# Moving a table build, two routings a tile and some opening work in a two-layer decoder kernel

## The reference, cut to what matters

```python
for l in range(2):
    h = rms_norm(x, norm1_g[l]);  q, k, v, f, u_pool, u_ssm = split(h @ w_in[l])
    att  = forgetting_attention(q, k, v, f)        # 8 heads x 64
    pool = multiscale_pool(u_pool)                 # windows 2, 4, 8, 16
    ssm  = s5(u_ssm)                               # 1024 complex states: s[t] = a*s[t-1] + b*u[t]
    x = x + concat(rms(att), rms(pool), rms(ssm)) @ w_out[l]
    h = rms_norm(x, norm2_g[l])
    for head in range(8):                          # "routing": product keys, top 16 of 128 x 128
        s1, s2 = scores(h @ w_q[l, head]);  e, gate = top16(top16(s1) + top16(s2))
        x = x + sum_k gate_k * gelu(h . u_tab[e_k]) * v_tab[e_k]
```

## Time and profile before

| what | value |
|---|---|
| median of 3 runs | 1547.77 us (1547.66 to 1549.18) |
| the profiled execution | 1547.98 us, of which span 1546.1 |
| busy: PE, DVE, ACT, POOL | 1049.1, 1083.2, 575.1, 619.7 us |
| moved by DMA | 623.55 MB, mean 403 GB/s |
| of that by the gathers' queue | 536.90 MB |

### The profile page before, as it was taken

One profiled execution on the slowest core, in us unless ns is written; L12 is line 12 of the kernel. 1 busy time (PEld: TensorE's weight loads), 2 busy tenths in 40 slices (PEclk: granted clock), 3 DMA queues, 4 the chain that ended last, 5 costly groups with the idle time before them and its releaser, 6 DMA issues. The chain is left out here.

```text
span 1546.1 us, 19439 instructions
## 1 busy us (share of the span) xinstructions
PE 1049.1 (68%) x6790; PEld 532.8 (34%) x6790; DVE 1083.2 (70%) x2485; ACT 575.1 (37%) x1768; POOL 619.7 (40%) x571
## 2 busy tenths in 40 slices
PE   8898656785854668776775667788588465565555
PEld 6685312333531334332552334333255111111111
DVE  8777998646999685654789767564579965444444
ACT  5544433623444433441544431354234432221222
POOL 0034345442753533443343433444243354455441
PEclk9999877887986988787897788889698777667767
DMA  9289999999999999999999999999999999999997
GB/s 381 89 326 421 420 421 420 421 421 405 422 421 368 411 422 421 421 421 421 409 421 421 421 421 421 421 422 420 422 386 421 421 421 422 421 421 422 421 421 304
DMA packets 86642, 623.55 MB, mean 403 GB/s; under 512 B 10000, under 2 KB 10128, under 8 KB 11792
## 3 DMA queue, kind: packets, MB, share of 16 engines
q0 software_dynamic: 73728, 536.90, 83.7%
q1 hardware_dynamic: 12816, 85.41, 13.4%
HBM read 621.23 MB, written 1.05 MB: 402 GB/s over the span
## 5 line engine op out<-in xcount | busy, mean ns | idle before, releaser
L583 POOL DMA_INDIRECT slots<-experts,idx x512 | 593.2, 1159 | 886.5 <-PE psum L1830 709.9
L1427 DVE CUSTOM_DVE_ANT_0 slots<-slots,h 128x1024 f32<-128x1024 f32 x512 | 615.9, 1225 | 390.8 <-DMA slots<-experts,idx 387.6
L1830 PE MATMUL psum<-slots,diag 64*64 64x512 f32 x4088 | 599.3, 737 | 312.4 <-ACT diag L947 312.3
L1830 PEld LDWEIGHTS psum<-slots,diag 64*64 64x64 f32 x4088 | 175.8, 165 | 684.2 <-ACT diag L947 368.9
L931 ACT ACTIVATE ge<-ge 128x4 f32<-128x4 f32 x130 | 26.7, 205 | 437.3 <-DVE ge L1427 436.3
L1752 PE MATMUL psum<-hT,ring 128*128 128x128 f32 x992 | 131.3, 297 | 20.7 <-DMA ring<-weights 16.0
L931 ACT ACT_TABLE_LOAD x55 | 70.6, 1283 | 194.7 <-DVE ge L1427 194.3
L947 ACT ACTIVATE diag<-cst,ge 128x64 f32<-128x64 f32 x511 | 136.5, 336 | 6.7 <-PE psum L1830 2.5
L1752 PEld LDWEIGHTS psum<-hT,ring 128*128 128x128 f32 x992 | 127.7, 212 | 23.5 <-issue 17.7
L938 ACT ACTIVATE ge<-ge,gate 128x1 f32<-128x1 f32 x512 | 109.1, 283 | 4.2
L1525 PE MATMUL psum<-ring,hT 128*128 128x256 f32 x192 | 52.2, 433 | 17.5 <-DVE work L981 17.5
(11 more groups left out here) (292 smaller groups left out, 1075.4 us busy)
## 6 DMA issues: line engine op xcount, KB each, us to landing
ring<-weights SPq DMA_DIRECT2D x32, 1152.0 KB, 10.0
ring<-weights SPq DMA_DIRECT2D x26, 1024.0 KB, 9.2
slots<-weights SPq DMA_DIRECT2D x11, 1024.0 KB, 20.0
slots<-experts,idx POOLq DMA_INDIRECT x512, 20.8
ring<-weights SPq DMA_DIRECT2D x2, 1056.0 KB
sml<-small SPq DMA_DIRECT2D x2, 652.0 KB, 9.1
slots<-weights SPq DMA_DIRECT2D x1, 1056.0 KB, 9.0
xs<-x SPq DMA_DIRECT2D x2, 512.0 KB, 13.2
```

The lines of the kernel that those rows point to most:

```text
L583: pool.indirect_dma_start(out=slot[:, place(E), :], out_offset=None, in_=src, in_offset=bass.IndirectOffsetOnAxis(ap=idx[:, n % 2, e:e + 1 ...
L1427: ins = dve.tensor_tensor_reduce(u, u, h2[:, n % 2, :], 1.0, 0.0, ALU.mult, ALU.add, d[:, i:i + 1])
L1830: ins = pe.matmul(acc[HALF * half:HALF * half + HALF, i, :], diag[rows, d % DIAGS, :], slot[rows, place(E), D + half * 512:D + half * 512 ...
```

## The change

Five things change.

1. `tab5`, `tab6`, `tab7` go from the rows of `route3` to `route5` (quads 28 to 30 of step 0) to those of `att0` to `att2` (quads 15 to 17). They now wait for the carries and for tile 1's `y`. The wait for the table goes from `normA` of step 2 to `sq` of tile 1 on ACT.
2. Every quad has at most one row, row q at quad q. `route6` and `route7` of tile n+1 leave step n; they stand at quads 2 and 4 of step n+1, with `normA` of the next tile at quad 1 and `normT` at quad 3. Quad 28 is left empty, so `route0` to `route2` are at quads 25 to 27 and `route3` to `route5` at quads 29 to 31. In steps 1 and 2 all later rows of the mixer up to `att2` come two quads later than before, the rest one.
3. In the opening ACT's 32 scalings for the output matrix (`mul0` to `mul3`, eight each) are spread: eight, then `cm`, then sixteen, and the last eight after `qkT`. DVE's `scan` is reordered: the reduction for q and k comes straight after `bu`, and the subtraction that was in `scan0` is a piece of its own, `scan_im`, after `qkn1`.
4. SP loads the first q chunk ahead of the constants, the drive table and the rest of the small parameters.
5. Tile 1's second projection, `qkv0` and `qkv1` stand ahead of tile 0's second routing.

```diff
+        "power4", "qkv0", "f", "prep", "fx", "ln", "mul0", "rotate0", "rotate1", "cum", "cm", "mul1", "mul2",
+        "qkv1", "rotate2", "bu", "qkv2", "qkv3", "qkn0", "scan0", "qkn1", "scan_im", "qkv4", "pool", "qkT", "pre0", "pre1",
+        "mixp", "mul3", "sq1", "scan1", "scan2", "scan3", "scan4", "scan5", "scan6", "logits0", "scan7", "big0", "logits1",
...
-        ("att0", "max0", "nrm0"), ("att1", "max1", "nrm1", "mixp"), ("att2", "max2", "nrm2"),
+        ("att0", "max0", "nrm0", "tab5"), ("att1", "max1", "nrm1", "mixp", "tab6"), ("att2", "max2", "nrm2", "tab7"),
...
+    if n == 0:
+        rows = [(1, r) for r in ((), ("qkn",), ("qkT", "v"))] + [(0, r) for r in ROUTES[2:]] + [(1, r) for r in MIX1]
+    elif n < STEPS - 1:
+        m = n + 1
+        rows = [EMPTY, (m, MIX[0]), (n, ROUTES[6]), (m, MIX[1]), (n, ROUTES[7])] + [(m, r) for r in MIX[2:]]
+    else:
+        return [EMPTY, (n, ROUTES[6]), EMPTY, (n, ROUTES[7])]
+    return rows + [(n + 1, r) for r in ROUTES[0:3]] + [EMPTY] + [(n + 1, r) for r in ROUTES[3:6]]
...
-            while at < len(rows) * (quad + 1) // QUADS:
+            at, rest = divmod(quad * GRP, 4)
+            step, row = rows[at] if rest == 0 and at < len(rows) else EMPTY
...
+            chunk(CH_Q)
             sp.dma_start(cst[:, P:], consts[:, P:]).then_inc(S["cst_in"], 16)
...
-                    sp.wait_ge(S["routed"], 2 * PH)
+                    sp.wait_ge(S["routed"], PH + 1)
...
                 if part == 5:
-                    pool.wait_ge(S["states_ready"], TILES)
+                    pool.wait_ge(S["carry_ready"], TILES)
+                    pool.wait_ge(S["y_psum"], TILES)
...
+            def scan_im(n):
+                link(tt(w3[1], w3[1], w3[3], ALU.subtract))
```

More of the change, by code:

```diff
@@ L84, with rows_of @@
        ("att1", "max1", "nrm1", "mixp"), ("att2", "max2", "nrm2"), ("att3", "max3", "nrm3"),
[2 rows of a table removed]
[1 row of a table added]
 MIX0 = ("warm", "dt", "power0", "normA", "power1", "normT", "inverse", "power2", "u", "uT", "p", "up", "power3",
[9 rows of a table removed]
[9 rows of a table added]
 MIX1 = (("bu",), ("scan",), ("backA",), ("backB",), ("y", "z"), ("glu", "pool"),
[1 row of a table removed]
+        ("att0", "max0", "nrm0", "tab5"), ("att1", "max1", "nrm1", "mixp", "tab6"), ("att2", "max2", "nrm2", "tab7"),
         ("att3", "max3", "nrm3"), ("att4", "attg", "sq"), ("merge", "out0"), ("out1", "x1a"),
[2 rows of a table removed]
-ROUTES = tuple((f"route{h}",) for h in range(1, PH))
+        ("out2", "x1p"), ("out3", "x1"), ("h2T", "rp"))
+ROUTES = tuple((f"route{h}",) for h in range(PH))
+EMPTY = (0, ())
+def rows_of(n):
+    if n == 0:
[6 more added lines that the diff above has]
+    return rows + [(n + 1, r) for r in ROUTES[0:3]] + [EMPTY] + [(n + 1, r) for r in ROUTES[3:6]]
 def script():
@@ L116, in script @@
     for n in range(STEPS):
[L117 to L122, removed]
-        at = 0
+        rows = rows_of(n)
         for quad in range(QUADS):
@@ L127, in script @@
                 order.append(("mix", "drain", n - 1))
-            done = at
-            while at < len(rows) * (quad + 1) // QUADS:
-                step, row = rows[at]
-                order += [("mix", s, 2 if s[:3] == "tab" else step) for s in row]
-                at += 1
+            at, rest = divmod(quad * GRP, 4)
+            step, row = rows[at] if rest == 0 and at < len(rows) else EMPTY
+            order += [("mix", s, 2 if s[:3] == "tab" else step) for s in row]
             order.append(("close", n, quad))
-            for step, row in rows[done:at]:
-                order += [("mix", "soft" + s[5:], step) for s in row if s[:5] == "route"]
+            order += [("mix", "soft" + s[5:], step) for s in row if s[:5] == "route"]
     for quad in (QUADS, QUADS + 1):
@@ L495, in _ @@
             rest_(0)
-            for i in range(6):
+            for i in range(1, 6):
                 chunk(CH_Q + i)
@@ L629, in normA @@
             def normA(n):
-                if n == TILES:
-                    act.wait_ge(S["rot_ready"], 2)
                 if n == 1:
@@ L838, in sq @@
                 if sec is None:
+                    if n == 1:
+                        act.wait_ge(S["rot_ready"], 2)
                     link(sq_sec(n, 1))
@@ L1116, in scan @@
                     link(tt(w3[0], w3[0], spare, ALU.add))
-                    link(tt(w3[1], w3[1], w3[3], ALU.subtract))
+                if part == 9:
+                    scan_im(n)
                 todo = [(r, b) for r in range(2) for b in range(SB)]
@@ L1428, in dots @@
                 told(ins, "dots_ready")
-            run(dict(inverse=inverse, fold=fold, attg=attg, x1p=x1p, x1a=x1a, h2=h2_, power=power, rotate=rotate_, normA=normA, normT=normT, uT=u_out, cum=cum,
+            run(dict(scan_im=scan_im, inverse=inverse, fold=fold, attg=attg, x1p=x1p, x1a=x1a, h2=h2_, power=power, rotate=rotate_, normA=normA, normT=normT, uT=u_out, cum=cum,
                      warm=blank, h2T=h2T, turnback=turnback, bu=bu, scan=scan, backA=back, backB=back_im, y=y_, glu=glu, qkn=qkn, qkT=qkT,
```

## The result

Five runs of each, taken together: before 1549.18 us (median; 1547.66 to 1553.06), changed 1556.89 (1556.24 to 1557.85). The ratio on record is 1.0057, 95% interval 1.0043 to 1.0071; it is not the quotient of the two medians, which is 1.0050 and lies inside the interval too. The forecast was 1547.6 with a range to 1553.5, so the time lies outside it. The profiled execution of the changed kernel has a span of 1555.1 us, 9.0 longer than before, for the same 623.55 MB.

A forecast was written before the change was run, and what follows sets the result against it. DMA engines taken as saturated: 623.55 MB over 421 GB/s is 1481 us, plus 65 us of holes. Terms - 2.0 - 5.9 + 6.1 + 1.6 = - 0.2 us gave 1547.6; range 1544.5 to 1550.5, with larger rivals 1543.0 to 1553.5.

The forecast's parts named there:

- parts 6 and 7: Table's later parts on POOL, beside attention rows: second hole, before E72's data, of 1.6 us (bounds 0 and 6.4).
- the table's first hole: Table's first part, behind E63 on POOL, delays E64: hole of 6.1 us (bounds 2.5 and 7.3).
- the opening: Before the first gather: earlier q and k reduction closes DVE's gap near 46 us, 2.0 us gained (bounds 1.2, 2.1).
- the end of step 0: Last routings of step 0: holes at 465 and 490 go, 5.9 us gained (bounds 3.6 and 5.9).
- the lower bound of 2.5: First hole at the table's new place if nothing on POOL waits for DVE: part takes 8.5 us, hole 2.5.
- The rival with the lock: Attention rows: table and dots shut each other out, holes of 7.4 and 6.4 us, time 1553.7; chance 0.25.
- the fourth rival: Rows `x1`: holes move with when weight chunks land, from - 2 to + 2 us, no preferred sign; no separate chance.

The follow-up runs named there:

- E72: Not a run: a gather POOL issues behind the table's part 7, 24.25 us after E64 in the changed kernel.
- narrow dots: The changed kernel with the dots of quads 15 to 17 taken over 8 of the 1024 columns; ratio 1.0012 to the kernel before.
- E68: Not a run: a gather POOL issues between E64 and E72, at 280.85 us in the changed kernel.
- E64: Not a run: the gather POOL issues behind the table's part 5, at 272.15 us in the changed kernel.
- E63: Not a run: the last gather POOL issues before the table's part 5, at 257.48 us; its dot on DVE waits for data until 268.43.

## Why the prediction was wrong, step by step

The sum was - 0.2 us and the spans differ by + 9.0. By the table above the error is made, rounded, of 4.0 us in parts 6 and 7, 2.2 in the table's first hole, 2.2 at `x1` and in the last stretch, for which the sum had no term, 0.6 in the opening and 0.4 at the end of step 0.

*The opening, - 2.0: 1.4 by the windows, and most of the gap had another cause.* Each of its times came (35.25 for the reduction, 46.05 for the first maximum, 84.30 for the first gather). But the gap of 2.04 us that the new order was to close is mostly not one of order. The kernel with the table alone moved has the old opening. Its reduction starts at 37.87, 0.09 later than before, and its first maximum nevertheless 1.57 earlier:

```profile
46.44 0.69 DVE L1211 TENSOR_REDUCE att_s<-psum 128x4 f32<-128x512 f32 x1 [0.38 <-PE psum L1602]
```

What differs is PE, which makes the logits. Its windows in the kernel before and in that one:

```profile
42.00:46.00 4.00, 4.00 (x22) 3.68 (x21) 3.80 (x11) 1.37 (x2) 0.00 (x0) 0.57 0.51 208
```

```profile
42.00:46.00 4.00, 4.00 (x37) 3.81 (x36) 3.83 (x11) 2.03 (x5) 0.00 (x0) 1.00 0.56 230
```

PE had been idle for 3.28 and 3.36 us just before. In the profiled execution of the kernel before its granted clock then fell (0.52 from 42 to 44, close to the 1.2 GHz level of 0.50), and in the other it stayed at 1.00, or 2.4 GHz. So some 1.7 of the 2.04 us belong to one execution's clock. The new order makes the opening safe against this: in the kernel with the opening alone the clock was at 0.56 from 42 to 44, and its first maximum came at 45.96 all the same. How much it gains depends on how often the clock falls with the old order, which two traces can't tell: the first gather went at 86.26 and 84.69 with the old order, and with the new one at 84.20 to 84.57 in eight traces and at 85.55 and 85.86 in two. The holes to 100 us are 43.0 and 42.0 with the old order and 40.6 to 43.0 with the new, so 1.4 is not clear of their spread, and the time of the opening alone gives 0.8 with an interval of 1.7 to either side.

*The end of step 0, - 5.9: the size right (- 5.5), the reason wrong.* The prediction gave the hole at 465 to the table and that at 490 to the second routing of quad 31. The runs show that neither stands when either cause is missing: both traces that have the two together show it (5.7 and 4.6 us), and the ten that lack one read 420 or 421 from 440 to 520. The table needn't have moved for it: this is the costliest error for a reader, since it makes the move look paid for.

*Parts 6 and 7, + 1.6: 5.6. This is the failed step: the overlap of the table's last part with the dots was priced at nothing in the 1.6 us.* Part 7 was taken at 7.0 from the earlier trace rows, where it was DVE that stood still beside it (the 6.56 us of the earlier trace rows), and took 9.1 from its first row to E72's issue, 6.9 with narrow dots. From E68 to E72 it was 15.55 us, 11.63 with narrow dots, whose second hole is 0.2 us: 5.4 of the 5.6 us are the lock's. E72 went 24.25 us after E64, not 21.6 to 22.9; by the prediction's own formula that is 24.25 + 1.7 - 22.4 = 3.6. Another 2 us are the slow start of E72's data (0.8 by the earlier trace rows) and a thin stretch from 302 to 306 us (322 GB/s over 4 us, 0.9), whose cause stays open. The prediction had all this in its upper bound (6.4) and took the value near the lower.

*The table's first hole, + 6.1: 8.3. The term that failed is the time at which the queue runs dry.* The lock was in this term, with 3.6 us of part 5, and E64's issue was forecast well: at 271.7 on the changed kernel's clock (273.7 less 2.0), and it came at 272.15. From there to the first bytes it took about the 1.7 us taken, as the window from 272 to 274 has 29 GB/s. But the sum took the start of E63's dot (270.09, 268.1 here) as a time up to which data flow at the full rate. They flow until 268.0, but ever thinner: what is lacking to 421 GB/s from 264 to 268 is 1.6 us. With the 0.45 us of E64 this is nearly the whole 2.2. In the kernel with narrow dots the rate falls in the same way ahead of the dot at 267.86, from 311 at 264.5 to 16 at 267, 1.8 us. This is also why the lower bound of 2.5 was too low: with part 5 at 9.0 us the hole is still 5.1 (the window from 260 to 280 at 313 GB/s, in the kernel with narrow dots).

*The rival with the lock* was the right case: 13.8 us of holes forecast, 13.8 measured, and the narrow dots take 8.5 of them away. That the two totals agree to the tenth is luck: its first hole was 7.4 and came out 8.3, though part 5 took 12.6 us and not its 13.4, and its second was 6.4 and came out 5.6. Its time, 1553.7, is 0.38% above the median of before; measured is 0.57%, and the difference of 3 us is what the opening and the end of step 0 fell short (0.6 and 0.4) and + 3.6 at `x1` of tiles 2 and 3 and in the last stretch, less 1.4 at `x1` of tile 1. What spoke against it, that dots paced by DMA leave half of DVE's time free, was true, but it is not the share of time that counts. POOL's instructions here are a chain of short ones, and each of the drawn-out ones ends just behind the dot that it met: the earlier trace rows showed a pair at 2.46 us, and the changed kernel has pairs at 1.25, 1.43, 1.54 and 1.77 in front of E64, where the kernel with narrow dots has 0.40, 0.45, 0.55 and 0.80.

*The holes of `x1`* moved as the fourth rival said, - 1.4 at tile 1 and + 2.2 at tiles 2 and 3. The holes at tiles 2 and 3 were 0.3 and 2.7 with the routings as before and the table at the end, 2.9 and 4.1 with the changed routings, but also 3.3 and 3.6 with the routings as before and the table early. What sets them stays open.

## What to carry to other kernels

Where the DMA engines are the bound and one engine both issues the gathers and computes, price a piece of computing by the data queued when it starts. Here the first byte came 1.7 us after an issue, and of the data up to the instruction that waits for the last gather 1.6 to 1.8 us were lacking, since the rate falls before the queue is empty. Beside an engine that was seen to hold it up take the drawn-out duration of the piece, and cut the piece so that each part fits into what issuing leaves free of a quad: here that alone took 0.5% off (1.0057 to 1.0006).

Before a move is credited with closing a hole, ask whether the other edit closes it alone. Before a gap is credited to the order of the program, look at the granted clock of the engine that it waits for: here it made 1.7 of 2.0 us. And look at what a wait that comes with a move will stop: 11.5 us here, for an engine that runs quads ahead.

## What the runs showed of the hardware

- When nothing is queued behind the last gather, the rate falls over 2.5 to 3 us and not at once: 262, 229, 213, 82, 49 GB/s in half-microsecond windows to 268.0 (dot at 268.43), and 311, 295, 246, 98, 16, 16 to 267.5 with narrow dots (dot at 267.86). The mean busy share of the engines falls with it, 0.62 to 0.12 in the first case.
- DVE on 8 columns took 2.61 us instead of 0.17 beside four back-to-back POOL instructions of 2.55 us together, and 5.85 us beside six of part 7. The issue of a gather is drawn out too: 1.97 us at 266.99, beside a dot at 266.87, instead of 0.94 (kernel with the table in five parts).
- With the same opening, PE's granted clock after an idle stretch of 3.28 us read 0.57 from 42 to 46, and after one of 3.36 us in another execution 1.00: 22 matmuls in the window against 37.
- In the first hole PE ran out of work (0.28 us busy from 268 to 272), and its granted clock then read 0.50, the 1.2 GHz level, from 272 to 280, and 0.50 again from 290 to 300, where before it was 0.89 over 260 to 320 (0.76 in the changed kernel). The matmuls of experts behind a hole so run at half the clock; how much of the 13.8 us is due to slots that were freed later was not measured.
